# One core: the stages ahead of the output projection in another order, the 96-row form four k at a time, and the form chosen ahead of the transposes

## What is computed

```python
mod = silu(c) @ w_ada + b_ada                      # 6 x 1024 columns ("ada"), for latent and context
hx  = rms_norm(x) * (1 + sc1) + sh1
px  = hx @ w_in                                    # q, f_fwd, f_bwd, values, gates, and 512 pooled columns
o_hg   = hgrn2_mixer(px[..., :2560])               # 4 heads of 128, a gated recurrence in both directions
o_pool = pool_mixer(px[..., 2560:])                # 4 groups; centred box means of 2, 4, 8, 16 on a 16 x 64 grid
x = x + gt1 * rms_norm(concat(o_hg, o_pool) @ w_out)
hx2 = rms_norm(x) * (1 + sc2) + sh2
top_val, top_idx = top_k(hx2 @ w_router + b_router, 4)      # of 32 experts
h = (clip(up) + 1) * min(gate) * sigmoid(1.702 * gate)      # gate, up = xb @ w_gate[e] + b, xb @ w_up[e] + b
x = x + gt2 * rms_norm(sum over the four experts of weight * (h @ w_down[e] + b_down[e]))
```

## Time and profile before

| what | number |
|---|---|
| time, median of 3 runs | 2658.65 us (2656.94 to 2666.75) |
| the profiled execution | 2663.03 us |
| its span | 2660.9 us |
| start (transposes, first ada units) | 0 to 57.3 us |
| four heads | 57.3 to 613.2 us |
| output projection, router | 613.2 to 773 us |
| tables, first items | 773 to 838.3 us |
| expert loop | 838.3 to 2613.9 us |
| tail (last down, final norm) | 2613.9 to 2660.9 us |
| busy: PE, DVE, ACT, POOL | 2438.0, 905.6, 497.9, 431.1 us |

### The profile page before, as it was taken

How to read it: one execution, slowest core, us unless ns; L and a number is a source line. 1 busy time by engine, 2 the same in 40 slices (tenths; PEclk the granted TensorE clock), 3 DMA queues, 4 the chain that set the end, 5 groups by cost and what they waited for, 6 DMA issues and landing times.

```text
span 2660.9 us, 35488 instructions
## 1 busy us (share of the span) xinstructions
PE 2438.0 (92%) x11660; PEld 1218.6 (46%) x11684; DVE 905.6 (34%) x1833; ACT 497.9 (19%) x1116; POOL 431.1 (16%) x368
## 2 busy tenths in 40 slices
PE   5999999967987899999999999999999999999992
PEld 3575766754553444444443343433444444334430
DVE  3154626472564222313222223223333323222224
ACT  4121222222442101101110102101111111010111
POOL 5000000003000121211222122222221212212123
PEclk9999999989985999999999999999999999999996
DMA  8112120206033868595899979979788898989875
GB/s 268 32 40 80 40 80 17 88 11 223 40 126 114 266 224 276 151 310 184 276 351 313 322 243 341 358 270 349 265 270 265 292 354 272 351 316 306 309 259 178
DMA packets 214858, 587.33 MB, mean 221 GB/s; under 512 B 20122, under 2 KB 79890, under 8 KB 214802
## 3 DMA queue, kind: packets, MB, share of 16 engines
q1 hardware_dynamic: 131650, 337.94, 34.8%
q10 hardware_dynamic: 55504, 197.22, 20.7%
q0 software_dynamic: 27648, 51.39, 9.5%
HBM read 548.20 MB, written 38.27 MB: 220 GB/s over the span
## 4 chain that ended last, share of the span: by engine, by line
PE 85%; DVE 8%; issue 3%; ACT 1%; POOL 1%; DMA 1%; DVEq 0%; ACTq 0%; POOLq 0%
PE ps L1658 24%; PE ps L1684 15%; PE ps L1714 12%; PE ps L1727 7%; PE ps L1418 4%; PE ps L1522 4%; PE ps L1414 3%; PE ps L1421 2%; PE ps L1478 2%; PE ps L1627 2%; PE ps L1424 1%; PE ps L1694 1%; PE ps L1390 1%; PE ps L1569 1%; PE ps L1676 1%
## 5 line engine op out<-in xcount | busy, mean ns | idle before, releaser
L1658 PE MATMUL ps<-w_gate_e,xT 128*128 128x512 f32 x736 | 346.5, 593 | 0.0
L1658 PE MATMUL ps<-w_up_e,xT 128*128 128x512 f32 x736 | 345.8, 592 | 0.0
L1714 PE MATMUL ps<-w_down_e,hT 128*128 128x512 f32 x736 | 319.8, 592 | 0.5 <-issue 0.5
L1272 DVE TENSOR_SCALAR oh_gu<-part_e,tab_e 128x128 bf16<-128x128 f32 x48 | 14.2, 297 | 870.3 <-PE ps L1658 551.8
L589 POOL DMA_INDIRECT xg<-xn_rows,gidx x49 | 50.7, 1035 | 1515.3 <-DVE sidx_tab L1263 1466.4
L845 ACT ACTIVATE sig_sb<-gate_sb 128x1024 f32<-128x1024 f32 x47 | 49.7, 1057 | 1167.1 <-DVE gate_sb L1278 1167.1
L1684 PE MATMUL ps<-w_gate_e,xT 128*32 128x256 f32 (+1 forms) x1504 | 238.3, 488 | 0.0
L1684 PE MATMUL ps<-w_up_e,xT 128*32 128x256 f32 (+1 forms) x1504 | 230.9, 475 | 0.0
L1658 PEld LDWEIGHTS ps<-w_up_e,xT 128*128 128x128 f32 x736 | 139.8, 190 | 176.0 <-issue 176.0
L1658 PEld LDWEIGHTS ps<-w_gate_e,xT 128*128 128x128 f32 x736 | 140.3, 191 | 169.0 <-issue 165.7
L1714 PEld LDWEIGHTS ps<-w_down_e,hT 128*128 128x128 f32 x736 | 138.0, 190 | 165.7 <-issue 165.7
(11 more groups left out here) (311 smaller groups left out, 2631.3 us busy)
## 6 DMA issues: line engine op xcount, KB each, us to landing
w_down_e<-in_w_down_dram ACTq DMA_DIRECT2D x368, 512.0 KB, 4.7
w_gate_e<-in_w_gate_dram SPq DMA_DIRECT2D x256, 512.0 KB, 5.1
w_up_e<-in_w_up_dram SPq DMA_DIRECT2D x256, 512.0 KB, 6.5
w_ring<-in_w_ada_dram SPq DMA_DIRECT2D x17, 1024.0 KB, 5.4
w_ring<-in_w_in_dram SPq DMA_DIRECT2D x20, 512.0 KB, 5.1
w_first<-in_w_ada_dram SPq DMA_DIRECT2D x7, 1024.0 KB, 12.4
x_all<-in_x_dram SPq DMA_DIRECT2D x2, 2048.0 KB, 10.4
w_out<-in_w_out_dram SPq DMA_DIRECT2D x8, 512.0 KB, 8.7
```

What stands on the lines that cost most here:

```text
L1658: last = T.matmul(ps[:, b, :], xT[:, k, :], wgt[b // 2][:, k, (b % 2) * 512:(b % 2) * 512 + 512], start=False, stop=k == KT - 1)
L1714: last = T.matmul(ps[:, 4 + b, :], hT[:, k, :], wgt[2][:, k, b * 512:b * 512 + 512], start=k == 0, stop=k == KT - 1)
```

## The change

1. **Forms of 96 rows.** `small_gate_up` and `small_down` take four k for one group of rows, then the same four for the other, then the next four k. The weights' semaphores are waited for in the first group and given back in the last.
2. **Loop order.** The transposes `hidden`, with the waits of the next gate/up, move behind the choice of form, one copy in each form's code. The numbers that choose the form and the expert, and the one for the second index column, are loaded behind the down products, ahead of the slot sums. The loop runs once less, its last passage is written out behind it.
3. **Heads.** The ada units are spread otherwise (3, 2, 2 in heads 0 to 2, nine in head 3, seven of them among the values), with another choice of ring buffers. The box means run between the batches of the scan, two groups in head 0 and two in head 1.
4. **POOL ahead of the tables.** The slot numbers are made once the last masks are used, not once all units are done; for that they lie where the masks lay. The writes of zeros into `y_dram` wait for `mod_ready`.
5. **Tables.** The last two `weigh` go to POOL. The first expert's number is the constant 0 (`item_expert` of item 0). DVE builds item 0's one-hot rows earlier and loads the number of the last item later.
6. **Start.** ACT and DVE leave the transposes' groups in another split, and the ada units are put 2, 3, 3 behind the three parts.

```diff
+        def chunk_before(n):
+            return max(m for m in range(n) if homes[m] == homes[n])
...
+        def values_and_ada(h, count):
+            vals, home = len(chunks), ring_home()
+            chunk([(w_in, 3 * HG + h * P, P), (w_in, 4 * HG + h * P, P)], [], home)
+            for t in range(NT):
+                units.append(("v", h, t, vals))
+                if t >= NT - count:
+                    n = rest_ada.pop(0)
+                    chunk([(w_ada, n * QW, QW)], [("a", n)], (home + 1 + len(chunks) % 2) % 3)
+            chunks[vals] = (chunks[vals][0], len(units))
+            return home
...
-            values(h)
-            by_levels.append(len(units))
             if h == 3:
+                values_home = values_and_ada(h, 7)
+                by_levels.append(len(units))
+                last_ada(values_home)
                 mixed(h - 1)
-            more_ada(1)
-            if h < 2:
-                forgets(h + 1)
-            more_ada(1)
-            if h < 3:
+                pooled(h - 2)
+            else:
+                values(h)
+                by_levels.append(len(units))
+                if h < 2:
+                    forgets(h + 1)
+                more_ada((3, 2, 2)[h])
                 queries(h + 1)
-            if h >= 2:
-                pooled(h - 2)
-            more_ada(2)
+                if h == 2:
+                    pooled(h - 2)
...
+        BOXES = ((0, 1), (2, 3), (), ())
...
+        X_ACT = [*range(KT), *range(2 * KT, 3 * KT, 2)]
+        X_DVE = [*range(KT, 2 * KT), *range(2 * KT + 1, 3 * KT, 2)]
+        X_UNITS = (range(0, 2), range(2, 5), range(5, n_ada_first))
...
             for n in range(KT + 2, len(chunks)):
-                chunk_is_used(sp, n - 3)
+                chunk_is_used(sp, chunk_before(n))
                 ring_load(n)
...
-            pool.wait_ge(proj_psum, len(units))
+            pool.wait_ge(lev_put, 2 * HEADS * LEVELS)
             link(G.memset(slot_ids[:], 0.5))
...
+            for t in range(TL - 2, TL):
+                weigh(t)
+            pool.sem_inc(weighed, 1)
...
+                box_parts = iter(())
+                for g in BOXES[h]:
+                    box_parts = itertools.chain(box_parts, box_means(g))
                 for j, (d, lo, hi) in enumerate(BATCHES):
...
-                for g in ((0, 1), (2,), (3,), ())[h]:
-                    box_means(g)
+                    next(box_parts, None)
...
+            def inverse_sum(t):
+                dve.wait_ge(top_exp, t + 1)
+                V.reciprocal(w_sum[:, t:t + 1], w_sum[:, t:t + 1]).then_inc(sum_inverse, 1)
...
-            def gate_up(m):
-                e = item_expert(pe, m)
+            def gate_up(m, e=None, v=None):
+                if e is None:
+                    e, v = item_expert(pe, m), item_variant(pe, m)
+                with pe.If(v == 3):
+                    hidden_and_free(m)
+                    whole_gate_up(m, e)
+                for some in (1, 2, 0):
+                    with pe.If(v == some):
+                        hidden_and_free(m)
+                        small_gate_up(m, e, PARTS[some])
+
+            def hidden_and_free(m):
+                if not (isinstance(m, int) and m < 1):
+                    hidden(m - 1)
                 pe.wait_ge(xT_ready, m + 1)
                 pe.wait_ge(oh_ready, m + 1)
                 if not (isinstance(m, int) and m < 1):
                     pe.wait_ge(gu_evac, m)
                 apart(pe)
...
-                for k in range(KT):
-                    pe.wait_ge(gu_in[k], e * 32 + 32)
-                    for lo, N, bank in parts:
-                        C = N * D // P
+                for k0, (lo, N, bank) in itertools.product((0, KT // 2), parts):
+                    C = N * D // P
+                    for k in range(k0, k0 + KT // 2):
+                        if bank == parts[0][2]:
+                            pe.wait_ge(gu_in[k], e * 32 + 32)
...
-            hidden(0)
-            with pe.Fori(0, n_last) as i:
-                gate_up(i + 1)
+            gate_up(1)
+            n_before = item_before_last(pe)
+
+            with pe.Fori(0, n_before) as i:
+                v_down = item_variant(pe, i)
                 rows(i + 2)
-                down(i)
-                slot_sums(i + 3)
-                hidden(i + 1)
+                down(i, v_down)
+                second = item_second(pe, i + 3)
+                e, v = item_expert(pe, i + 2), item_variant(pe, i + 2)
+                slot_sums(i + 3, second)
+                gate_up(i + 2, e, v)
+            rows(n_last + 1)
+            down(n_before)
+            slot_sums(n_last + 2)
+            hidden(n_last)
             down(n_last)
```

More of the change, by code:

```diff
@@ L576, in _, with weigh @@
             G.tensor_copy(bias_pc[2 * NE:3 * NE], bias_rows[2 * NE:3 * NE]).then_inc(pieces, 1)
+            def weigh(t):
+                pool.wait_ge(sum_inverse, t - TL + 3)
+                link(G.tensor_scalar(w_route[:, t, :], w_route[:, t, :], w_sum[:, t:t + 1], None, ALU.mult))
+                link(G.tensor_scalar(w_full[:, t, :], iota_e[:], top_f[:, t, 0:1], w_route[:, t, 0:1], ALU.is_equal,
+                                     ALU.mult))
+                for j in range(1, TOP_K):
+                    link(G.tensor_scalar(oh_j[:, t, :], iota_e[:], top_f[:, t, j:j + 1], w_route[:, t, j:j + 1],
+                                         ALU.is_equal, ALU.mult))
+                    last = G.tensor_tensor(w_full[:, t, :], w_full[:, t, :], oh_j[:, t, :], ALU.add)
+                    if j < TOP_K - 1:
+                        link(last)
+                last.then_inc(w_full_ready, 1)
+                pool.wait_ge(w_full_ready, t + 1)
+                rest = w_full
+                for piece in range(3):
+                    part = rtab_bf[:, t, 3 + piece * NE:3 + (piece + 1) * NE]
+                    link(G.tensor_copy(part, rest[:, t, :]))
+                    if piece < 2:
+                        link(G.tensor_tensor(rtab[:, t, :], rest[:, t, :], part, ALU.subtract))
+                        rest = rtab
+            for t in range(TL - 2, TL):
+                weigh(t)
+            pool.sem_inc(weighed, 1)
             for k in range(2):
@@ L710, in turned @@
             def turned(part):
-                for g in range(part * KT, (part + 1) * KT, 2):
+                for g in X_ACT:
+                    if g // KT != part:
+                        continue
                     k, t0, nt, _ = XGROUPS[g]
@@ L926, in turned @@
             def turned(part):
-                for g in range(part * KT + 1, (part + 1) * KT, 2):
+                for g in X_DVE:
+                    if g // KT != part:
+                        continue
                     k, t0, nt, _ = XGROUPS[g]
@@ L1443, in turn @@
                     last.then_inc(xt0_psum, 1)
[L1445 to L1450, removed]
+            for part in range(len(XPARTS)):
+                turn(part)
+                run(X_UNITS[part])
             ada_columns()
@@ L1702, in down @@
                 apart(pe)
-                v = item_variant(pe, m)
+                if v is None:
+                    v = item_variant(pe, m)
                 with pe.If(v == 3):
                     whole_down(m)
-                for some, parts in enumerate(PARTS):
+                for some in (1, 2, 0):
                     with pe.If(v == some):
-                        small_down(m, parts)
+                        small_down(m, PARTS[some])
             def whole_down(m):
@@ L1718, in small_down @@
             def small_down(m, parts):
-                for k in range(KT):
-                    pe.wait_ge(dn_in[k], m * 16 + 16)
-                    for _, N, bank in parts:
-                        C = N * D // P
+                for k0, (_, N, bank) in itertools.product((0, KT // 2), parts):
+                    C = N * D // P
+                    for k in range(k0, k0 + KT // 2):
+                        if bank == parts[0][2]:
+                            pe.wait_ge(dn_in[k], m * 16 + 16)
                         at, kk = divmod(k, KT * N // P)
@@ L1737, in _ @@
                 first_rows(t)
+            pe.wait_ge(weighed, 1)
             slot_sums(0)
```

64 lines of the change are left out of this document (38 added, 26 removed).

## The result

The changed kernel takes 2581.32 us (median of 4 runs, 2578.18 to 2584.12) against 2660.07 (4 runs, 2656.94 to 2666.75): ratio 0.9705, interval 0.969 to 0.9721, or 78.7 us less. The forecast was 2563, its range 2535 to 2598. The profiled runs stand 84.4 us apart (2663.03 and 2578.59). Single runs of one kernel scatter by 6 to 10 us, and part of that lies ahead of every changed instruction: in six kernels with the start of before, the first product of head 0 came between 126.1 and 131.3 us.

What follows compares the result with a forecast made beforehand. TensorE was taken as the bound, busy 1701.2 of the expert loop's 1775.6 us. Terms of -52.8 (loop), -26.9, -13.4, -1.1 and -1.6 sum to -95.8 from the median 2658.65: 2563 us, range 2535 to 2598.

Steps and rivals of the forecast that it cites:

- Part 1: Loop's mixed 96-row forms: four k at a time saves 1.81 us a gate/up, 1.62 a down; -30.8 us.
- Part 2: Loop order: gaps ahead of bias matmuls -30 us, items with 32-row groups +5, slower clock -2, first code passages +5.
- tables -1.1: Table stage: about 0.45 us from two `weigh` taken off VectorE and 0.65 for a load left out.
- rival (c): Loop: the branch to a form's code must fetch it, uncovered; 6.27 us once, +288 at 46 items, 2851; chance 0.04.
- Part 3: Heads: box means between scan batches -20.4 us, with ada units spread otherwise -26.9 in all (-20 to -31).
- Seven go into its levels: +1: Head 3: seven ada units in levels where TensorE waits 1.2 to 2.8 us each for VectorE cost only +1.
- Part 4: Output stage: early slot numbers let POOL's bias pieces come 11.4 to 12 us earlier; -13.4 us (-10 to -16).
- Part 5: Table stage -1.1 us; start -1.6 (0 to -3), with ada units ahead of the wait for the last transposes.
- rival (e): Table stage: POOL's weights come late, +6 us, 2569; counted inside the forecast's chance of 0.72.
- (a): Loop: the gap moves instead of going, since loads wait for the queue to empty; +30 us, 2593; chance 0.12.
- (b): Loop's mixed forms: the excess is in each small matmul, not at group boundaries; no gain there, 2594 us; chance 0.08.
- (d): Loop: DMA becomes the bound, for a pair of mixed items at most; +1 to +5 us; inside the forecast's 0.72.

Runs made afterwards that it cites:

- The alone run: The kernel before with only the loop's order on TensorE changed (transposes behind the choice of form, numbers loaded ahead of the slot sums): 2634.55 us, ratio 0.9913.

## Why the prediction was right in sum and wrong in the heads

**Part 1 (the 96 forms): right.** The excess was at the boundaries. Forecast 1.81 and 1.62 an item, measured 1.73 and 1.73. It gave more in all (37.8 us for both against 30.8), because the slow gate/ups, as the one of 24.60 in the earlier trace rows, vanished but for one.

**Part 2 (form ahead of the transposes): right in place and in sum.** I read 56.5 us of gap as idle; 5.2 of them were bias matmuls without a record. By the windows above TensorE's idle time in the loop fell from 72.2 to 44.9 us; less those 5.2 that is 22.1, and my terms for it (-30, +5, +5) come to -20. The alone run gave 25.0; with the -2 for the clock the terms come to -22. The gap behind mixed downs that I expected at 1 to 2 us is 1.6 to 1.7. The first passages: branches of over 1 us came to 20.8 us after against 15.8 before, +5 as put down. But one of them has no cover: the term "tables -1.1" became +3.8 since the branch of 4.9 us ahead of item 0 stood behind a wait. I had costed the edit of `gate_up` for the loop and not for its call ahead of it. This is rival (c) on a small scale. The Trainium skill ("Runtime: NRT & Kernel Launch", Instruction fetch mechanics) has such a stall for a branch out of the fetched window; the trace agrees: the branches of over 1 us come at first passages only, and the median of the 141 stays at 0.20.

**Part 3 (heads): the step that failed.** Three terms. (1) Head 1 was to win 0.4 us net by the pieces; it lost 6.4 in two waits. I had taken the planner's cost of 7 us for every forget unit. Its third part has 256 columns and takes 3.5, so the second piece had 5 us of cover instead of 8.5. The last long piece I had 2.1 late, it was 3.4. The run with the pieces handed out otherwise shows it: both waits gone, 7.7 us back in head 1. (2) "Seven go into its levels: +1" was +3.3: the waits of L1478 and L1414 in head 3 came to 11.6 us before and 4.1 after, so 7.5 of 10.8 us of units were covered; a unit covers a wait only where the two meet. (3) The slow clock, the largest in head 3: I let 3 us of slow matmuls go, and counted none that come. TensorE's busy time in head 3 rose from 80.3 to 91.5 us, 7.7 of it the five units more, so 3.5 us came instead. Head 3's mean granted clock went from 0.97 to 0.93; the wait of 2.8 us for the last ada chunk, forecast at 3.3, is followed by the same matmuls at twice the time:

```profile
575.56 1.07 PE L1470 MATMUL ps<-w_ring,cT 128*32 128x256 f32 x16
...
579.97 1.93 PE L1470 MATMUL ps<-w_ring,cT 128*32 128x256 f32 x16 [2.80 <-DMA w_ring<-in_w_ada_dram]
```

In sum head 3 took 7.9 us more instead of 1.8 less, head 1 took 0.8 more instead of some 5 less. Heads 0 and 2 (-5.3 and -13.4) were near the forecast.

**Part 4 (slot numbers): right, 1.7 low.** I had TensorE wait 2 us for the pieces. The loads landed 3.3 us after their issue, not up to 10.9 as in the earlier trace rows, POOL began as the last landed, and the pieces were done 1 us into the output stage; the transposes (L1531 before) had no wait:

```profile
609.08 1.80 POOL L607 MEMSET bias_pc<- 128x2048 bf16 x1 [28.34 <-DMA bias_rows<-in_b_up_dram]
...
625.08 1.88 POOL L614 CAST bias_pc<-bias_rows 32x2048 bf16<-32x2048 f32 x1
```

**Part 5: start too small, tables too good.** The start gave 4.6 in the profiled run; I had counted the ada units and not that TensorE's three waits of 4.7 us between its transposes go with them (to 1.9). The weights on POOL took 10.6 us and were done 15 us before the slot sums: rival (e) didn't come.

**The rivals.** (a) The gaps went: it didn't come. (b) It is out by the straight line. (c) It came at the first passages only. (d) No wait for a weight stands in the changed kernel.

## What to carry to other kernels

Cover work with work by the measured length of each piece at its place; a planner's cost per kind hid a unit of half the length, and the two waits in head 1 cost 6 us here. Where loads of numbers and branches stand in a matmul queue, put them behind the matmuls that last longest, few in a row: turning two groups round gave 21.8 us, four loads in a row cost 11.6, half of it as waits. A branch to code that is reached for the first time shows in full when it stands behind a wait (a gap of 7.16 us, 2.28 with the choice ahead of the wait); the choice belongs ahead of the wait.

## What the hardware showed that I had not expected

A change between matmul groups of 64 and 32 columns costs 0.144 us, the mean of both directions (15, 7 and 3 of them lie on one line). First branches into code not yet run took up to 8.6 us on TensorE's queue, 3 to 6 of them over 1 us in every kernel here. And idle time in the view of waits can hold a matmul whose record is missing, 0.23 us in each of 23 items: the count of records by form shows it.
